# Attention values and modulation column sums with two 64-column stationary halves instead of one of 128

## What is computed

```python
c_act = jax.nn.silu(c)
shift, scale, gate = jnp.split(c_act @ mod_w[i] + mod_b[i], 3, axis=-1)
h = _rms_norm(x, norm_g[i]) * (1.0 + scale[:, None, :]) + shift[:, None, :]
...
# forgetting attention, 16 heads of 64
p = jax.nn.softmax(jnp.where(causal, logits, -jnp.inf), axis=-1)
outs.append(jnp.einsum('bhqk,bhkd->bhqd', p, v[:, :, :qe]))
...
# dilated window attention, 8 heads of 64
out = jnp.einsum('bdnhqk,bdnkhe->bdnqhe', p, vc) / s.transpose(0, 1, 2, 4, 3, 5)
```

## Time and profile before

| | before |
|---|---|
| median of 3 runs (lowest to highest) | 717.03 us (716.78 to 717.21) |
| profiled execution | 714.63 us |
| its span, first to last instruction | 712.8 us |
| mean granted TensorE clock | 0.994 |
| PE busy | 698.2 us, 98% of the span |
| PE weight loads busy | 581.5 us, 82% |
| DVE busy | 499.9 us, 70% |
| ACT busy | 377.6 us, 53% |
| DMA | 139.11 MB, 195 GB/s in the mean |

### The profile page before, as it was taken

One profiled execution on the slowest core, in us unless ns is written; L12 is line 12 of the kernel. 1 busy time (PEld: TensorE's weight loads), 2 busy tenths in 40 slices (PEclk: granted clock), 3 DMA queues, 4 the chain that ended last, 5 costly groups with the idle time before them and its releaser, 6 DMA issues.

```text
span 712.8 us, 9664 instructions
## 1 busy us (share of the span) xinstructions
PE 698.2 (98%) x3694; PEld 581.5 (82%) x3694; DVE 499.9 (70%) x726; ACT 377.6 (53%) x553; POOL 16.2 (2%) x33
## 2 busy tenths in 40 slices
PE   6999999999999999999999999999999999999996
PEld 5889997777888888788888888878888888888885
DVE  4888988787956778665768889855865545555445
ACT  5457434565545665554656754555575454444344
POOL 6001000000000000000000000000000000000000
PEclk8999999999999999999999999999999999999999
DMA  9999775666986267733445643432556655665611
GB/s 298 368 381 378 256 238 182 201 210 223 305 300 206 96 200 253 248 119 107 158 133 165 197 128 119 146 118 93 167 184 199 186 183 174 193 190 182 200 62 59
DMA packets 74493, 139.11 MB, mean 195 GB/s; under 512 B 5732, under 2 KB 18384, under 8 KB 74448
## 3 DMA queue, kind: packets, MB, share of 16 engines
q1 hardware_dynamic: 72816, 134.92, 58.2%
q10 hardware_dynamic: 736, 1.81, 0.7%
q0 software_dynamic: 896, 1.77, 0.7%
HBM read 137.44 MB, written 1.05 MB: 194 GB/s over the span
## 4 chain that ended last, share of the span: by engine, by line
PE 92%; DVE 4%; ACT 2%; DMA 1%; issue 1%; SPq 0%; DVEq 0%; ACTq 0%
PE G L382 23%; PE G L384 23%; PE G L383 22%; PE T L423 5%; PE T L784 2%; PE T L900 2%; DVE wlo L1074 1%; PE G L402 1%; PE T L774 1%; PE G L404 1%; PE G L403 1%; DMA arena<-in_mod_w_dram 1%; PE G L513 1%; PE G L515 1%; PE G L514 1%; DVE arena L1083 1%
## 5 line engine op out<-in xcount | busy, mean ns | idle before, releaser
L1074 DVE TENSOR_TENSOR wlo<-raw,whi 128x1024 fp32r<-128x1024 f32 x202 | 246.0, 1222 | 120.4 <-ACT whi L1840 119.7
L1840 ACT ACTIVATE whi<-raw 128x1024 fp32r<-128x1024 f32 x202 | 212.8, 1060 | 135.1 <-PE G L384 93.6
L382 PE MATMUL G<-whi,ahi 128*128 128x512 f32 x696 | 281.6, 405 | 0.4 <-DVE wlo L1074 0.4
L384 PE MATMUL G<-whi,alo 128*128 128x512 f32 x696 | 272.2, 391 | 0.0
L383 PE MATMUL G<-wlo,ahi 128*128 128x512 f32 x696 | 271.4, 390 | 0.0
L382 PEld LDWEIGHTS G<-whi,ahi 128*128 128x128 f32 x696 | 130.9, 188 | 28.3 <-DVE wlo L1074 2.3
L384 PEld LDWEIGHTS G<-whi,alo 128*128 128x128 f32 x696 | 130.7, 188 | 28.4
L383 PEld LDWEIGHTS G<-wlo,ahi 128*128 128x128 f32 x696 | 131.2, 188 | 25.8 <-issue 1.2
L1842 ACT ACTIVATE arena<-T,st 128x128 f32<-128x128 f32 (+2 forms) x56 | 21.6, 476 | 30.4 <-DVE st L1459 30.4
L402 PE MATMUL G<-ahi,whi 128*128 128x256 f32 x128 | 36.5, 285 | 0.9 <-DVE wlo L1074 0.9
L1840 ACT ACTIVATE ahi<-T 128x512 fp32r<-128x512 f32 x25 | 14.9, 597 | 41.9 <-PE T L423 41.9
(11 more groups left out here) (237 smaller groups left out, 666.4 us busy)
## 6 DMA issues: line engine op xcount, KB each, us to landing
raw<-in_ret_w_in_dram SPq DMA_DIRECT2D x48, 512.0 KB, 5.4
raw<-in_w_gate_up_dram SPq DMA_DIRECT2D x40, 512.0 KB, 3.6
raw<-in_mod_w_dram SPq DMA_DIRECT2D x32, 512.0 KB, 4.8
raw<-in_fox_w_in_dram SPq DMA_DIRECT2D x32, 512.0 KB, 4.9
raw<-in_w_in_dram SPq DMA_DIRECT2D x28, 512.0 KB, 3.6
raw<-in_w_down_dram SPq DMA_DIRECT2D x22, 512.0 KB, 4.3
arena<-in_mod_w_dram SPq DMA_DIRECT2D x16, 512.0 KB, 9.6
raw<-in_ret_w_out_dram SPq DMA_DIRECT2D x16, 512.0 KB, 5.9
```

The source lines that it names most:

```text
L382: e.matmul(o, ah, wh, start=first and k == 0, stop=False)
L384: done = e.matmul(o, al, wh, start=False, stop=last and k == 1)
L1074: e.tensor_tensor(o, a, b, op).then_inc(sig[name], 1)
L1840: d = e.activation(o, a, f, scale=scale)
```

## The change

Each of four products is cut into two halves of 64 stationary columns. The first half (`c` = 0) writes partitions 0 to 63 of the same PSUM columns as before, the second (`c` = 64) partitions 64 to 127. The moving operand is the same for both. The order of the groups, the waits and the semaphore updates stay; the update hangs on the second half of the last product.

```diff
             def own_rows(g, i, a):
 
                 r0 = VECTOR_ROWS[g]
+                o = sums_of(SUMMED[g][i], a)
                 for r in range(r0, 8):
-                    e.matmul(sums_of(SUMMED[g][i], a), mod_tile(g)[:, a, r, i * P:(i + 1) * P], cact[:, r:r + 1], start=r == r0, stop=False)
+                    for c in (0, 64):
+                        e.matmul(o[c:c + 64, :], mod_tile(g)[:, a, r, i * P + c:i * P + c + 64], cact[:, r:r + 1], start=r == r0, stop=False)
 
             def other_rows(g, i, a):
 
                 on_.wait_ge(sig["macc"], g + 1)
-                return e.matmul(sums_of(SUMMED[g][i], a), macc[:, g % 2, a, i * P:(i + 1) * P], ones[:, 0:1], start=False, stop=True)
+                for c in (0, 64):
+                    d = e.matmul(sums_of(SUMMED[g][i], a)[c:c + 64, :], macc[:, g % 2, a, i * P + c:i * P + c + 64], ones[:, 0:1], start=False, stop=True)
+                return d
...
                 for j in range(4 * part, 4 * part + 4):
-                    d = e.matmul(t[:, j:j + 1], acc[:, j * P:(j + 1) * P], ones[:, 0:1], start=True, stop=True)
+                    for c in (0, 64):
+                        d = e.matmul(t[c:c + 64, j:j + 1], acc[:, j * P + c:j * P + c + 64], ones[:, 0:1], start=True, stop=True)
...
                     for j in range(m + 1):
-                        d = e.matmul(t[:, 65 * a:65 * a + 65], PT[:, g % 2, (a * (m + 1) + j) * P:(a * (m + 1) + j + 1) * P],
-                                     v[:, j, h, :], start=j == 0, stop=j == m)
+                        c0 = (a * (m + 1) + j) * P
+                        for c in (0, 64):
+                            d = e.matmul(t[c:c + 64, 65 * a:65 * a + 65], PT[:, g % 2, c0 + c:c0 + c + 64], v[:, j, h, :], start=j == 0, stop=j == m)
```

## The result

The changed kernel takes 712.76 us in the median of 4 runs (712.54 to 712.90), the kernel before 717.12 us (716.78 to 718.44, 4 runs): ratio 0.9937, 95% interval 0.9922 to 0.9951, 4.4 us less. The sign and the mechanism are those of the forecast; the gain is twice its size.

The account below looks back on a forecast made before the run. PE was taken to bound the kernel after 100 us, saturated DMA the first 55 us. Gains of 1.8 (values), 0.4 (line 606) and 0 (shift and scale) made 2.2 us: 717.03 to 714.8 us, range 713.6 to 720.5.

Parts of the forecast that it names:

- PE bounds the kernel behind 100 us: After 100 us PE waits only 0.8 us in all, so PE time saved in attentions and line 606 shortens the kernel.
- A 128-column load costs 0.111 us, a pair of 64-column loads 0.058: In the changed products, two 64-column loads run at a time; a group of 8 loads saves 0.42 us on loads.
- The row halves of L774: Loads alternating between two 64-row halves start 0.052 us apart, two at a time; column halves were assumed to behave so.
- In and out of the split array cost 0.33 us: At each group of values and line 606, changing mode gives back 0.33 us; a group goes from 1.13 to 1.03 us.
- The sum of 2.2: Total gain in us: 1.8 from values, 0.4 from line 606, 0 from shift and scale.
- Later three stretches of shift and scale: Column sums in the first layer, 16 loads each: PE saves 0.5 us each but waits for `alo`, so gain 0.
- First two stretches: Shift and scale sums at 9.8 and 18 us: results 0.5 and 1.2 us earlier, but weights wait for DMA; gain 0.
- The median of the runs is 717.03: Whole kernel: the median has the profiled execution's stages, so the 2.2 us gain comes off 717.03, giving 714.8 us.
- 1: Changed products: the halves run one after the other, 0.116 us per pair, giving 726.1 us; chance 0.16.
- Rivals 2 and 3: Changed products: pairs at 0.087 us, 720.3 us, chance 0.15; or array not split, no holes, 717.9 us, chance 0.04.
- Rival 4: New holes in PE's work might lower the clock; no size given; chance 0.03 together with anything else.
- What would show it wrong: Evenly spaced loads, pairs above 0.07 us, no holes, or an L513 at 52 us earlier by 0.5 us or more.

Follow-up runs that it names:

- the late part alone: Halves only in the values of both attentions and the sums of line 606, against the kernel before: 714.81 us, ratio 0.9963.
- the second profile: Profile of the kernel before, unchanged and run again: span 715.6 us, 2.8 more than its first profile; median 717.52 us, ratio 1.0001.
- quarters: The changed kernel with the column sums in four parts of 32 stationary columns, the values still in halves: 712.16 us, ratio 0.9924 to the kernel before.
- the reordered kernel: The kernel before with the next row product put ahead of the second stretch of sums and 8 idle transposes behind them: 718.05 us, ratio 1.0011.

## Why the prediction was wrong, point by point

- **PE bounds the kernel behind 100 us; a microsecond there is one of the kernel.** Right: the late part alone gains 2.4 us, and PE's trace is shorter by 2.3.
- **A 128-column load costs 0.111 us, a pair of 64-column loads 0.058.** Right, by 16 loads in 0.55 us. The row halves of L774 were the right model.
- **In and out of the split array cost 0.33 us, 0.10 us per group remain.** Right for the values of the first attention (0.10); 0.075 in the second, 0.16 at line 611. There the load of L382 comes 0.15 us behind the last pair of loads, behind the values 0.20; that one moving column in place of 65 does this is my reading and not tested. The sum of 2.2 was 2.3.
- **Later three stretches of shift and scale: nothing.** Right. The L517 load near 41 us follows a hole of 0.81 us where the earlier trace rows has 0.23, so PE's saving there became idle time, 0.6 us of it for the forecast 0.5:

```profile
41.69 0.19 PEld L517 LDWEIGHTS G<-whi,ahi 128*128 128x128 f32 x1 [0.81 <-issue]
```

- **First two stretches: 0, with bounds of 0 and 1 us.** This is the term that was mis-sized: 1.8 to 2.0 us. The reason to count it at nothing was sound in the execution that was read, where ACT waits for the memory. It doesn't hold in the second profile, where these sums and the products behind them run at 1.2 GHz and PE is above the floor; there the second stretch alone is 1.7 us shorter by the halves (4.1 to 2.4), where the prediction had 1.2. The times say that most executions are of this kind.
- **"The median of the runs is 717.03, 2.4 us longer, and its stages are the same."** This is the step that failed. The two profiles of before differ in one stage: by 2.6 us, all before 36 us. There the sums at 18 us and the products behind them run at half clock and PE is the last to be ready, and the change shortens just these sums, from 4.1 to 2.4 us, which brings PE back to the floor. So 2.0 of the 2.4 us were not to be added on behind the gain. The sum itself, made against the profiled execution (712.4 us), came within 0.3 us of the changed kernel's profiled time (712.71), and the changed kernel's median is 712.76. That this works although the clock was low until 18.8 us in the one execution and until 25.3 in the other is owed to the floor, on which both stand.
- **Rivals.** 1 did not happen, but the kernel with both halves in one place shows that its price (8 us) was right. The Trainium skill, "TensorE: Matmul & The Clock Gate", section The mechanism, says that a weight load overlaps running matmuls only where the row group differs; here loads of two column halves over the same rows start 0.006 to 0.007 us apart in the single records of the group shown above, and the measurement decides. (The 2.38 times for three column tiles, which the prediction puts in the same section, stands in that page's section Measured speedup vs the span model.) Rivals 2 and 3 did not happen: pairs are at 0.058, and the holes are there. Rival 4, the clock, was given little because the new holes are short; the place where it seems to matter was not the new holes but the first 30 us, and the sign was a gain.
- **What would show it wrong** named an earlier L513 at 52 us. Beside the first profile nothing is earlier; beside the second profile of before the product of weights near 34 us is, by 2.4 us (33.97 and 36.42). One trace of before was not enough to see it.

What stays open: why the clock comes back at 18.8 us in one execution of the kernel before and at 27 in another (the attempt to force it changed the order as well), how the 1.8 us divide between the first two stretches, and what makes the slower kind of before at 719 us.

## What to carry to other kernels

When the profiled execution is faster than the median of the runs, here by a third of a per cent, ask where the median's extra time lies before adding it on: look for the stage where the clock or the memory can differ between executions, and take the gain there as unknown up to that whole difference. For products with few moving columns (1 and 65 here) the loads set the pace, and two or four column parts of the array load side by side; the way into and out of the split is paid once per group (some 0.3 us here), so put groups that use a split next to each other (0.17 to 0.18 us per group here). A part that stands on a floor of the memory takes no gain beyond it: in the second stretch quarters took another 1.0 us of PE's work away and the kernel was not earlier.

## What the runs showed of the hardware

- Four quarters of 32 columns load at the same time: 32 float32 loads in 0.35 us, against 0.55 for 16 in halves and 0.97 for 8 whole ones.
- Two halves in the same place of the array run one by one, 0.058 us each; in two places they cost 0.058 per pair.
- The stretch at 1.2 GHz early in the program differs between executions of one kernel: products of 512 columns take 0.63 us until the clock rises, at 18.8 us in one and at 27.0 in another. In the first the clock rose 0.8 us into the column sums, behind products of the whole array (L513 to L515); in the other it stayed down through all the sums and rose only 4.7 us behind them, among such products; in the reordered kernel it fell again at 23.1 us, when 8 transposes behind the sums ended.
- In one execution of the changed kernel a low clock at 16 us is shown by the products' durations (0.63 us) and not by the granted clock (1.00).
- Changing from the whole array to column halves and back costs some 0.3 us at a group of values: a hole of 0.17 us in the loads ahead (behind transposes) and of 0.15 behind.
